# Moving the modulation products of a two-block kernel to GpSimd

## The reference, cut to what matters

```python
m  = jnp.split((jax.nn.silu(c) @ w_ada[l] + b_ada[l])[:, None, :], N_MOD, axis=-1)
mc = jnp.split(jax.nn.silu(c_ctx) @ w_ada[l] + b_ada[l], N_MOD, axis=-1)
```

## Time and profile before

| | us |
|---|---|
| median of 3 runs | 3298.45 (3293.58 to 3306.25) |
| the profiled execution | 3298.1 |
| its span, first to last instruction | 3296.0 |
| TensorE busy in it | 2972.9 (90%) |
| VectorE busy | 1391.3 (42%) |
| ScalarE busy | 1081.7 (33%) |
| GpSimd busy | 35.4 (1%) |
| mean granted TensorE clock | 0.944 of full |

### The profile page before, as it was taken

How to read it: one execution, slowest core, us unless ns; L and a number is a source line. 1 busy time by engine, 2 the same in 40 slices (tenths; PEclk the granted TensorE clock), 3 DMA queues, 4 the chain that set the end, 5 groups by cost and what they waited for, 6 DMA issues and landing times.

```text
span 3296.0 us, 44230 instructions
## 1 busy us (share of the span) xinstructions
PE 2972.9 (90%) x15161; PEld 2511.1 (76%) x15161; DVE 1391.3 (42%) x2309; ACT 1081.7 (33%) x1597; POOL 35.4 (1%) x27
## 2 busy tenths in 40 slices
PE   6999989899998999968999999499978899599997
PEld 5778777689877778848999999378756577387785
DVE  4335444556644333354323323744444334533334
ACT  3223455332223222234213112422443344442322
POOL 0000000000000000000000000000000000000000
PEclk9999999899999999989999999799989899799997
DMA  3224211344444343421121221011100023133332
GB/s 102 64 76 128 58 51 53 86 123 115 138 133 130 102 115 109 133 70 45 57 64 58 61 60 57 19 39 37 38 19 16 21 67 99 45 90 89 89 90 63
DMA packets 479232, 247.90 MB, mean 75 GB/s; under 512 B 15289, under 2 KB 477578, under 8 KB 479034
## 3 DMA queue, kind: packets, MB, share of 16 engines
q1 hardware_dynamic: 479162, 247.01, 26.3%
HBM read 244.88 MB, written 2.10 MB: 75 GB/s over the span
## 4 chain that ended last, share of the span: by engine, by line
PE 69%; issue 19%; DVE 6%; ACT 4%; DVEq 1%; ACTq 1%; DMA 0%; POOL 0%; POOLq 0%; SPq 0%
PE unit_acc L659 61%; PE aux L862 2%; PE aux L1060 2%; PE aux L1084 1%; PE aux L644 1%; ACT w_hi L1169 1%; DVE w_lo L1655 1%; PE aux L973 1%; PE aux L671 1%; DVE ssq L1673 1%; DVE x L2054 1%; DVE mla_stat L2255 1%; ACT h_hi L1206 1%; PE aux L955 1%; DVEq L2052 0%
## 5 line engine op out<-in xcount | busy, mean ns | idle before, releaser
L659 PE MATMUL unit_acc<-h_hi,w_hi 128*128 128x512 f32 (+2 forms) x2816 | 888.5, 361 | 65.3 <-DVE h_lo L1693 40.3
L659 PE MATMUL unit_acc<-h_lo,w_hi 128*128 128x512 f32 (+2 forms) x2816 | 865.6, 353 | 0.0
L659 PE MATMUL unit_acc<-h_hi,w_lo 128*128 128x512 f32 (+2 forms) x2816 | 864.4, 353 | 0.0
L1655 DVE TENSOR_TENSOR w_lo<-raw,w_hi 128x1024 fp32r<-128x1024 f32 (+3 forms) x405 | 484.8, 1197 | 601.2 <-ACT w_hi L1169 600.2
L1169 ACT ACTIVATE w_hi<-raw 128x1024 fp32r<-128x1024 f32 (+3 forms) x405 | 419.5, 1036 | 905.2 <-PE unit_acc L659 831.9
L659 PEld LDWEIGHTS unit_acc<-h_hi,w_hi 128*128 128x128 f32 x2816 | 504.9, 191 | 156.1 <-issue 52.2
L659 PEld LDWEIGHTS unit_acc<-h_hi,w_lo 128*128 128x128 f32 x2816 | 507.2, 191 | 56.6
L659 PEld LDWEIGHTS unit_acc<-h_lo,w_hi 128*128 128x128 f32 x2816 | 508.5, 191 | 50.3
L659 PE MATMUL unit_acc<-branch_hi,w_hi 128*128 128x512 f32 x448 | 181.8, 406 | 8.0 <-DVE branch_lo L1980 8.0
L659 PE MATMUL unit_acc<-u_hi,w_hi 128*128 128x384 f32 (+1 forms) x528 | 165.4, 368 | 23.0 <-DVE u_lo L2071 23.0
L659 PE MATMUL unit_acc<-branch_lo,w_hi 128*128 128x512 f32 x448 | 180.9, 404 | 0.0
(11 more groups left out here) (285 smaller groups left out, 3095.4 us busy)
## 6 DMA issues: line engine op xcount, KB each, us to landing
raw<-in_w_in_dram SPq DMA_DIRECT2D x132, 512.0 KB, 3.9
raw<-in_ffn_w_dram SPq DMA_DIRECT2D x120, 512.0 KB, 3.8
ada_raw<-in_w_ada_dram SPq DMA_DIRECT2D x72, 512.0 KB, 4.8
raw<-in_w_up_dram SPq DMA_DIRECT2D x32, 512.0 KB, 4.8
raw<-in_w_down_dram SPq DMA_DIRECT2D x32, 512.0 KB, 3.7
raw<-in_w_branch_dram SPq DMA_DIRECT2D x24, 512.0 KB, 3.9
raw<-in_w_out_dram SPq DMA_DIRECT2D x16, 512.0 KB, 3.7
raw<-in_ffn_w_dram SPq DMA_DIRECT2D x16, 384.0 KB, 3.2
```

The lines of the kernel that those rows point to most:

```text
L659: last = pe.matmul(G[s][0:n, 512 * j:512 * j + m], w[s][:, k, 0:n], x[:, k, a:a + m], start=(k == 0 and i == 0), stop=(k == kc - 1 and i = ...
L1655: dve.tensor_tensor(wl[s][:, 0:kc, :], raw[s][:, 0:kc, :], wh[s][:, 0:kc, :].bitcast(F32), ALU.subtract).then_inc(lo_split, 1)
```

## The change

All 72 chunks take one way. GpSimd multiplies the whole 128 x 1024 chunk by silu of the condition (broadcast along the 128 columns), halves the sum three times (512, 256 and 128 elements) and leaves a 128 x 128 sum per condition, one or two of them; TensorE multiplies each by a column of ones; VectorE copies one or two columns into `ada`. The chunks are numbered in the order they are worked: 0 to 7 in retention (two a head, loaded behind the loads of units 3 and 5), 8 to 39 in the merges and the convolution, 40 to 63 in parts one to three of the feed-forward (steps behind up units 2, 4, 6 and down units 0, 1, 3, 5, 7), 64 to 71 in the last part (one load behind each up load; steps behind up units 1 to 7 and down unit 0). `ada_unit`, VectorE's `ada_products` and the loads in the output projection go. `ada_raw` keeps its two buffers; there is one product buffer and one sum per condition, so GpSimd waits for the copy of the chunk before (`ada_out`). The up and down loops are unrolled over the 8 units. The additions that make gains from `ada` move into the last part's first down iteration, and VectorE's context copies wait for the last chunk's sum.

```diff
+            def ada_products(j, both):                       # GpSimd
+                pool.wait_ge(ada_landed[j.slot],
+                             val(Count(16 * (j.base // 2) + 16, *((r, 8 * st) for r, st in j.terms))))
+                pool.wait_ge(ada_out, val(j + 1))
+                alone(pool, pool_passed)
+                for e in range(both):
+                    if e:
+                        pool.drain()
+                    pool.tensor_tensor(aprod[:, :, :], araw[j.slot][:, :, :],
+                                       silu_c[:, :, e:e + 1].to_broadcast([P, KC, P]), ALU.mult)
+                    for n in (4, 2):
+                        pool.drain()
+                        pool.tensor_tensor(aprod[:, 0:n, :], aprod[:, 0:n, :], aprod[:, n:2 * n, :], ALU.add)
+                    pool.drain()
+                    last = pool.tensor_tensor(asum[e][:, :], aprod[:, 0, :], aprod[:, 1, :], ALU.add)
+                last.then_inc(ada_used, 1)
...
             with pool.Fori(0, RET_H) as h:
+                ada_products(Count(0, (h, 2)), 2)
                 pool.wait_ge(r_var, val(Count(1, (h, 1))))
                 pool.tensor_tensor(rpow[:, :], rvar[:, :], minus_half[:, 0:NT], ALU.pow).then_inc(r_pow, 1)
+                ada_products(Count(1, (h, 2)), 2)
...
+            def ada_step(j, both):                           # TensorE
+                pe.wait_ge(ada_used, val(j + 3))
+                pe.wait_ge(ada_out, val(j + 1))
+                alone(pe, pe_passed)
+                for e in range(both):
+                    last = pe.matmul(A[1][:, 512 + e:513 + e], asum[e][:, :], ones[:, 0:1], start=True, stop=True)
+                last.then_inc(ada_mm, 1)
...
                 unit(u + 5, HH, HL, GM)
+                ada_step(Count(1, (h, 2)), 2)
                 pe.wait_ge(r_y, val(Count(1, (h, 1))))
...
+            def ff_up(part, final):                          # TensorE
+                for n in range(KC):
+                    unit(count(U_FF + n, (part, 16)), HH, HL, GM, ready=(ap_lo, KC))
+                    if final:
+                        if n:
+                            ada_step(Count(ADA_ALL - KC + n - 1), 1)
+                    elif n in (2, 4, 6):
+                        ada_step(Count(ADA_BOTH + n // 2 - 1, (part, 8)), 1)
...
+            for n in range(KC):                              # SP, last part
+                load_up(FF1 // D - 1, n)
+                load_ada(Count(ADA_ALL - KC + n))
...
+            def ada_copy(j, both):                           # VectorE
+                dve.wait_ge(ada_mm, val(j + 1))
+                alone(dve, dve_passed)
+                dve.tensor_copy(ada[:, bass.ds(j.value(), 1), 0:both], A[1][:, 512:512 + both].unsqueeze(1)).then_inc(
+                    ada_out, 1)
...
+                    dve.tensor_tensor(BL[:, n, :], sqb[1][:, 0:SEQ], BH[:, n, :].bitcast(F32),
+                                      ALU.subtract).then_inc(ff_lo, 1)
+                    if final:
+                        j = Count(ADA_ALL - KC + n)
+                        if n:
+                            ada_copy(j + -1, 1)
...
+            dve.wait_ge(ada_used, ADA_ALL + 2)
             for c in range(KC):
                 dve.wait_ge(ctx_done, c + 1)
                 dve.tensor_copy(X2[:, c, 0:CTX], A[c % 2][:, 0:CTX]).then_inc(ctx_out, 1)
```

More of the change, by code:

```diff
@@ L513, in load, with load_ada @@
                     raw_landed[u.slot], 16)
-            def load_ada(q, chunk):
+            def load_ada(q):
                 sp.wait_ge(ada_used, val(q + 1))
@@ L733, in _ @@
                 retention(h)
[L735 to L739, removed]
             def merge(r):
@@ L852, in _ @@
                         unit(Count(U_CONV + 3 * e + k, (i, 6)), HH, HL, G1 if k else GM)
-                    ada_step(Count(ADA_STEP_CONV + e, (i, 2)))
+                    ada_step(Count(ADA_STEP_CONV + e, (i, 2)), 2)
             merge(2)
[L856 to L863, removed]
@@ new lines, in ff_down @@
+            def ff_down(part, final):
+                for n in range(KC):
+                    pe.wait_ge(ff_lo, val(count(8, (part, 8))))
+                    unit(count(U_FF + 8 + n, (part, 16)), BH, BL, GS)
+                    if n == 0:
+                        ada_step(Count(ADA_ALL - 1) if final else Count(ADA_BOTH + 3, (part, 8)), 1)
+                    if not final and n % 2:
+                        ada_step(Count(ADA_BOTH + 4 + n // 2, (part, 8)), 1)
+            last_part = FF1 // D - 1
@@ L888, in _ @@
+            with pe.Fori(0, last_part) as part:
+                ff_up(part, False)
+                ff_down(part, False)
+            ff_up(last_part, True)
             pe.wait_ge(ctx_in, 32)
@@ new lines, in ff_down @@
+            def ff_down(part, final):
+                for n in range(KC):
+                    u = count(U_FF + 8 + n, (part, 16))
+                    done(u)
+                    x = X[:, n, META:T1]
+                    dve.tensor_tensor(x, acc(G[u.slot], GS), x, ALU.add).then_inc(evicted[u.slot], 1)
+                    split(u + 2)
+                    if final:
+                        add_in_turn(ssq[:, 0:SEQ], sqb, SEQ, 0, n)
+                    if n == 0:
+                        ada_copy(Count(ADA_ALL - 1) if final else Count(ADA_BOTH + 3, (part, 8)), 1)
+                        if final:
+                            ada_gains()
+                    if not final and n % 2:
+                        ada_copy(Count(ADA_BOTH + 4 + n // 2, (part, 8)), 1)
```

179 lines of the change are left out of this document (77 added, 102 removed).

## The result

The changed kernel takes 3423.64 us (median of four runs, 3417.13 to 3425.09) against 3296.01 for the one before: ratio 1.0369, 95% interval 1.0353 to 1.0386, so 3.7% slower. The forecast was 3376, in a range of 3310 to 3450: the sign and the range held, the size fell 48 us short. The profiled execution took 3417.13 us around a span of 3415.3, which is 119.0 more than that of before (3298.1), where the sum had said 78. These are the rows of its page that answer to the earlier trace rows: busy time by engine, then the chain of waits.

What follows compares the result with a forecast made beforehand. TensorE was taken as the bound, busy 2972.9 of 3296.0 us. Removed products -62, ones products +16, retention +44, merges +27, middle feed-forward +5, last part +48 make +78 on 3298.1: 3376 us, range 3310 to 3450.

Steps and rivals of the forecast that it cites:

- Removed products, -62: TensorE drops 40 chunks' direct products; 35 at 1.77 us gain 62 us, five only lengthen waits already there.
- A vector of 4.7 us, a pair of 9.7: GpSimd's time for one chunk's vector or two, at 2.15 ns an element plus drains; bounds 2.7 to 7.2 us a vector.
- Retention, 44: Odd chunks' products start behind GpSimd's pow: 9.0 us stall in 4 heads, 36, plus 8 for the lower clock.
- Merges, 27: Copy, products and step miss the next step by 1.9, 2.5 and 3.25 us in the three merges; 27 us of stalls.
- The convolution, 0: Three units to a step and a later copy hide GpSimd's products: 0 us, at most 20.
- the prologue, 0: Stretch up to the first unit: the sum had no cost there, 0 us.
- rival 4: GpSimd holds VectorE up: splits 1.1 us late 24 times, 26 us more, 3402 us; chance 0.11.
- Feed-forward parts 1 to 3, 5: Most steps hidden; only down units 0 and 1, a unit apart, stall 1.65 us in each of three parts: 5 us.
- Last part, 48: Feed-forward's last part, a chunk per unit: stalls of 48 us, context copy at 98.1 us after part three's last down unit.
- the ring: Last part: sum, SP's queued loads, raw weight, split, branch_lo, copy and products form a closed chain, 14.2 us a turn against 5.8.
- (1): Rival 1: GpSimd's two-operand pace equals the copy's, merges and middle parts hide all, 3312 us; chance 0.14.
- (2): Rival 2: the last part's ring does not close because loads run ahead, 16 us instead of 48, 3344 us; chance 0.11.

Runs made afterwards that it cites:

- run 2: Changed kernel with two sum buffers per condition, so GpSimd's products wait for the copy of two chunks before: 3317.14 us, ratio 1.0057.
- run 6: Kernel before plus 60 scratch GpSimd vectors from the feed-forward's first branch_lo on: 3301.03 us against 3297.33, ratio 1.0009.
- Run 9: Kernel before with seven of eight direct products of each of the 40 chunks left out: 3239.12 us against 3304.59, ratio 0.9805.
- Run 3: Changed kernel with the retention's modulation steps put one place later, off the place right behind GpSimd's pow: 3381.09 us, ratio 1.0239.
- run 5: Changed kernel with two sum buffers, later retention steps, earlier last-part w_up loads, and GpSimd's first product held until the prologue's normalisation ends: 3278.64 us, ratio 0.9935.
- Run 1: Changed kernel with each last-part w_up load put one chunk earlier in SP's queue, ahead of the modulation load: 3406.95 us, ratio 1.0316.
- run 4: Kernel before plus 120 scratch GpSimd vectors from the end of the differential heads, awaited only by the context copies: 3455.68 us, ratio 1.0478.
- run 8: Changed kernel with two sum buffers, later retention steps and earlier last-part w_up loads, GpSimd's first product not held: 3274.34 us, ratio 0.991.
- run 7: Changed kernel without the 1024-element product, so modulation vectors lack silu(c) and GpSimd's vector is shorter: 3317.97 us, ratio 1.0059.

## Why the prediction was right, and what was mis-sized

**The direction and its cause: right.** What GpSimd does costs little by its own amount (runs 2 and 6); what it does late costs 115.7 us of stalls, and the clock behind them.

**Removed products, -62: right.** Run 9 puts them at 65 in the stages where they stand; in the changed kernel those up to the last part gave 48.7, where the sum had 49.6. The waits that were to swallow five chunks did lengthen: the sum of squares' from 2.89 to 4.57 us, the first down unit's from 2.65 to 4.44.

**A vector of 4.7 us, a pair of 9.7: right.** A product takes 1.90 us, the adds 1.26, 0.72 and 0.45, a drain 0.14 (0.2 was put), and a vector 4.76 in all; a pair beside one split 10.5 where 10.9 was put. The bracket from the copies held: 1.86 ns an element for the product with a broadcast operand, between the lone copy's 1.08 and twice that.

**Retention, 44: right.** It cost 40.1 beyond its ones products. 36.4 are stalls (forecast 36), of which other waits give 3.4 back; TensorE's busy time grows by 7.1 beyond the ones products, the clock (forecast 8). Run 3 takes 43 back.

**Merges, 27: the step that was mis-sized.** They cost 54.2 (run 2), and half of the miss and more is a cost that the term left out. The mechanism of the stalls, every second pair short by the shortage, is what the trace shows; the shortages were 1.8, 2.4 and 4.2 (6.1 the first time) for 1.9, 2.5 and 3.25. In the third merge the chain is longer since GpSimd's own adds are held up: the final add of a vector took 1.29 and 1.25 us there beside VectorE, and 0.46 a pair later. The rest is TensorE's clock. Here are busy times in merge 0, in heads and merge 1, and in convolution and merge 2, of the changed kernel and then of run 2 (us, then PE, PEld, DVE, ACT and POOL busy; the number behind the POOL column is the granted clock):

```profile
287.04:396.98 109.94, 102.34 (x425) 81.75 (x425) 30.64 (x37) 33.23 (x34) 73.87 (x64) 0.93 0.38 105
396.98:783.83 386.85, 344.44 (x1944) 279.81 (x1944) 159.82 (x408) 168.21 (x403) 82.59 (x72) 0.92 0.23 66
783.83:1058.35 274.52, 250.78 (x1408) 219.43 (x1409) 111.38 (x128) 67.00 (x80) 159.96 (x128) 0.94 0.38 106
```

```profile
285.74:385.01 99.27, 96.44 (x426) 78.58 (x426) 38.59 (x37) 33.24 (x34) 81.43 (x64) 0.98 0.42 116
385.01:756.36 371.35, 338.34 (x1944) 275.88 (x1945) 167.97 (x408) 168.22 (x403) 91.91 (x72) 0.94 0.24 69
756.36:1002.81 246.45, 239.98 (x1409) 210.75 (x1409) 137.65 (x128) 67.03 (x80) 178.98 (x128) 0.99 0.42 119
```

For the same matmuls TensorE is busy 697.6 us in the one and 674.8 in the other: 22.8 us go to the lower clock, for which the prediction's term for the merges had nothing; it charged the clock to the retention alone. TensorE's idle time differs by 31.4, the stalls of 35.4 less 4.0 by which other waits are shorter. So stalls make 4 of the missing 27, and the clock 23. Busy times after a stall of 1.77 and after one of 4.18:

```profile
314.94:318.50 3.56, 3.53 (x12) 2.78 (x13) 0.99 (x2) 0.00 (x0) 2.25 (x2) 0.62 0.44 131
978.17:981.70 3.53, 3.53 (x10) 2.98 (x11) 0.57 (x2) 0.00 (x0) 1.90 (x1) 0.50 0.75 218
```

So the engine can fall to the lower of its two levels (1.2 GHz) after an idle time of 1.8 us too, and in these stretches a stall costs 1.4 (3.56 x 0.38) and 1.8 us (3.53 x 0.50) on top of itself, 1.9 on the mean of the twelve (22.8 / 12). Not every such idle time does it: in the differential heads waits of 1.76 and 2.65 us, at 455.70 and 487.88, were followed by 4 us at a granted 1.00.

**The convolution, 0, and the prologue, 0: small misses.** With the hand-over loosened (run 2) the merges, heads and convolution still take 17.9 us more than before. Of that, 6.4 are the second ones products. Of the other 11.5, TensorE's idle time makes 3.2 (2.0 of it a wait for a split at the convolution's end) and its busy time 8.2, in part at the lower clock (0.98 in merge 0 for 1.00). The contention that rival 4 named can be behind it, but no run measures that apart. In the prologue the first pair meets VectorE's sums of squares, on VectorE's timeline

```profile
26.67 2.24 DVE L1716 TENSOR_TENSOR ssq<-ssq,square 128x528 f32<-128x528 f32 x1
...
31.38 3.29 DVE L1716 TENSOR_TENSOR ssq<-ssq,square 128x528 f32<-128x528 f32 x2
```

which take 0.71 and 1.51 in the kernel before. The first unit is 4.1 us late, 0.6 of it from before GpSimd's start; with the pair held back (run 5) it is at 38.5 again. No step of the prediction asked what GpSimd's first product runs beside.

**Feed-forward parts 1 to 3, 5: too small.** The stall behind down unit 1 is 2.81 and not 1.65, three times, and the three down stretches together take 14.2 us more than before. Without the ones products that is 11 us for the 5: 8.4 of stall, and 2.8 that the sum left out here too.

**Last part, 48: right.** The context copy came 99.2 us after the end of part three's last down unit, for 98.1 forecast. Run 1 shows that the ring passes through SP's queue, and run 2 that its other half, the one sum buffer, suffices to open it.

**The rivals.** GpSimd was not fast (1), the ring did close (2), the vector was as sized (3). Rival 4 exists but elsewhere: run 4 shows it at +155 us, with VectorE's own drained products in the way, and run 6 at nothing. By the Trainium skill (SBUF — State Buffer, § Who interferes with whom) the port pair is a lock between VectorE instructions with two inputs in SBUF and GpSimd's that read SBUF; run 4's rows agree (352 to 818 ns with both tensors on chip, 691 to 692 with one in the accumulator). Run 6 adds that a queue with slack does not pay for it. With the hand-over loosened one more place pays: in runs 2, 5 and 8 TensorE waits 7.6 to 7.7 us for the first `h_lo` of the feed-forward, 5.0 before. The prediction valued the removal of VectorE's products at nothing. That it makes room for a GpSimd that holds VectorE up is likely from runs 2 and 4 together; no run has both the products on VectorE and a GpSimd paced as in the changed kernel.

## What to carry to other kernels

When work moves to an idle engine, write down for each hand-over what must be over before it may start, and add up the chain copy, work, use, copy against the time between two uses; a second buffer for the small result was worth 106 us here, as much as taking two fifths of the work out of each vector (run 7). Count the clock with each stall, short ones too. Put free-running work on the engine before trusting an argument about contention, once where its neighbour's queue is full and once where it has slack, and read in the first case which of the neighbour's operations the bottleneck waits for.

## What the runs showed that was not expected

- Three edits turn the change from 3.7% slower to 0.9% faster than before (3274.34 us, 0.9885 to 0.9936), with all 72 chunks on GpSimd.
- GpSimd beside VectorE: a split of 1.23 us took up to 2.96 (run 5), a drained product of 0.35 us 0.82 on average (run 4); an operation that reads the accumulator was not stretched.
- The same GpSimd load cost 155 us over 713 in one stretch, and 4 (interval -2 to 9) over 360 in another.
- An idle time of 1.77 us on TensorE was followed by 3.6 us at a granted clock of 0.62, and one of 2.65 us elsewhere by 4 us at 1.00. In the merges the clock cost nearly as much as the forecast had for the stalls (22.8 us; 27).
